# A forward part added first, a backward part scaled sooner, two buffers for B and C, and exponentials of 512 columns whose column terms TensorE sums, in the chunks of a bidirectional state-space mixer

## The chip, the cores and the metric

The program runs on 1 core of one Trainium2 chip. The metric is the device time of one execution in microseconds (us). A core has a matrix engine (TensorE, PE in the rows; PEld is its weight load), a vector engine (VectorE, DVE), an activation engine (ScalarE, ACT), a general engine (GpSimd, POOL) and a queue engine that starts most transfers (SyncE, SP). Each runs its own instructions in the order in which they are written, and they wait for one another by semaphores. Data lie in SBUF (128 partitions); TensorE writes to the eight banks of PSUM, each of 512 float32 columns.

## The reference, cut to what matters

The model has two layers over a sequence of 1024 tokens of width 1024. In each layer a state-space mixer, a gated mixer and an attention mixer read one normalised input; their outputs are joined, projected and added, and a convolutional feed-forward part follows. The change touches the state-space mixer. It works in chunks of 128 tokens, once forward and once backward, for 8 heads in 2 groups:

```python
def ssd_chunked(x, dt, a_neg, bm, cm):
    ...
    acs = jnp.cumsum((dt * a_neg).reshape(b, nc, q, g, hg), axis=2)
    seg = acs[:, :, :, None] - acs[:, :, None, :]
    decay_in = jnp.exp(jnp.where(tri[:, :, None, None], seg, NEG_INF))
    cb = jnp.einsum('bctgn,bcsgn->bctsg', cc, bc)
    y_diag = jnp.einsum('bctsg,bctsgh,bcsghp->bctghp', cb, decay_in, xdt)
    ...
    y_off = jnp.einsum('bctgn,bcghpn,bctgh->bctghp', cc, prev, jnp.exp(acs))
    return (y_diag + y_off).reshape(b, s, g, hg, p)

def ssd_mixer(xbc, z, dt_raw, conv_w, conv_b, dt_bias, a_log, d_skip, out_gain):
    ...
    y_fwd = ssd_chunked(xs, dt[:, :, 0], a_neg[0], bm, cm)
    y_bwd = flip(ssd_chunked(flip(xs), flip(dt[:, :, 1]), a_neg[1], flip(bm), flip(cm)))
    y = y_fwd + y_bwd + d_skip.astype(jnp.float32).reshape(SSD_GROUPS, hg)[..., None] * xs
    y = y.reshape(b, s, SSD_INNER) * jax.nn.silu(z.astype(jnp.float32))
    ...
```

For a chunk and a head, the exponent is a table of 128 x 128: a term of the row, a term of the column, and minus infinity where the one token may not see the other. Four such tables (the heads of a group in one direction) fill one bank of PSUM.

## The kernel before, in words

The stage that the change touches comes after attention in each layer (about 384 to 475 us in the first layer, 1611 to 1702 us in the second). First the seven backward links are computed (ra_turn, ra_state on TensorE, state_in and the loop after it on VectorE), which leaves the backward states of all chunks in BW. In the same stretch tables for the exponents are made: rows_twice writes log terms to PSUM, ScalarE copies them to MHL, and far on VectorE writes FAR (the masks) and the low halves of MHL. Then the eight chunks run in order, one after the other, each with work on four engines:

- TensorE, function chunk: the products with the carried states CURF (forward) and BW (backward), L1081, into banks 5 and 6; the exponents of group 1, which are sums(n, 2) and sums(n, 3) (each is one matrix product with FAR, L1059, and one with MHL, L1064, both over 512 columns); the gated mixer's products, L1089 and L1092; the transposes and B-C products of the next chunk, L1048 and L1051; the state of this chunk, L1104; the exponents of group 0 of the next chunk, sums(n+1, 0) and sums(n+1, 1); and last the product of the weighted table SEG with XS, L1116, one half for each group.
- ScalarE: it copies XS (L1601) and BC (L1605) out of PSUM, takes the exponentials into SEG (L1613, one instruction for each head, direction and group, as the bias differs: 16 in a chunk, of 128 columns), scales a part of the gated mixer (L1591), scales the backward product to Y2 (L1623, 8 instructions), and takes sums of squares of the chunk before (L1583).
- VectorE: it scales the forward product to Y1 (L2149) and the carried state (L2151), multiplies the gated part (L2157), then for each group adds both directions of SEG (L2143) and multiplies by the B-C table (L2144), adds the new state (L2164), and closes the chunk with L2173 and L2175.
- GpSimd, function scan: it weights XS to XW (L655), which the state product L1104 reads, makes Y3 from XS (L657), adds Y2 (L660) and then Y1 (L665); L2173 waits for the sum.

Nothing but this written order and the semaphores decides when an instruction runs; there is no planner. Chunks are called 0 to 7 here, and chunk n has n = 0 to 7. Of buffers, SEG and XS are there twice, BC, XW, Y1, Y2 and Y3 once. The second half of L1116 waits for the second L2144 (semaphore w_masked), and the next chunk's L1081 stands behind it on TensorE.

Of the kernel before, what the change touches and what calls it, by code (L numbers as in the profile page):

```python
# [19 lines left out]
F32 = mybir.dt.float32  # L20
# [5 lines left out]
P = 128  # L26
# [131 lines left out]
def trunk(nc, xT, xtok, wst, params, consts, onehot, lnrow, table, outT):  # L158
# [12 lines left out]
    with ExitStack() as ctx:  # L171
# [96 lines left out]
        ZG = place("ZG", [P, 2, 3, UC], u_at + 8192)  # L268
        JUNK = place("JUNK", [P, GROUPS, 256], u_at + 16384)
# [25 lines left out]
        BC = work("BC", [P, 2, GROUPS, P])  # L295
# [294 lines left out]
        def _(pool):  # L590
# [56 lines left out]
            def scan(l):  # L647

                for c in range(NT):
                    n, xs = l * NT + c, by_head(XS[:, c % 2])  # L650
                    pool.wait_ge(xs_ready, n + 1)
                    if c < LINKS:
                        if c:
                            pool.wait_ge(sf_full, l * LINKS + c)
                        nc.gpsimd.tensor_tensor(by_head(XW[:]), xs, per_head(WST[:, c, 0:8]), ALU.mult).then_inc(xw_ready, 1)  # L655
                    pool.wait_ge(chunk_done, 1 + n)
                    step.then(nc.gpsimd.tensor_tensor(by_head(Y3[:]), xs, per_head(par_("d_skip")), ALU.mult))  # L657
                    if c < LINKS:
                        pool.wait_ge(y2_ready, l * LINKS + c + 1)
                        ins = nc.gpsimd.tensor_tensor(Y3[:], Y3[:], Y2[:], ALU.add)  # L660
                        if c:
                            step.then(ins)
                    if c:
                        pool.wait_ge(y12_done, 1 + l * LINKS + c)
                        ins = nc.gpsimd.tensor_tensor(Y3[:], Y3[:], Y1[:], ALU.add)  # L665
                    ins.then_inc(y3_ready, 1)
# [19 lines left out]
        def _(pe):  # L686
# [167 lines left out]
            for l in range(DEPTH):  # L854
# [165 lines left out]

                def tile_in(i):
                    pe.wait_ge(xbs_full[i % 4], 16 * (l * (6, 6, 2, 1)[i % 4] + i // 4 + 1))
# [16 lines left out]
                for i in range(2, LINKS):  # L1039
                    tile_in(i)  # L1040
                    ra_turn(i)
                    pe.wait_ge(ra_t_full, l * LINKS + i + 1)
                    pe.sem_inc(xbs_used, 1)
                    ra_state(i - 1)

# [21 lines left out]

                def chunk(i2, par, end):
# [27 lines left out]
                    if not end:  # L1096
# [6 lines left out]
                        for g in range(GROUPS):  # L1103
                            last = nc.tensor.matmul(PS[:, 7, g * 256:(g + 1) * 256], BC[:, 0, g, :],  # L1104
                                                    XW[:, g * 256:(g + 1) * 256], start=True, stop=True)
# [169 lines left out]
        def _(act):  # L1275
# [121 lines left out]
            for l in range(DEPTH):  # L1397
# [154 lines left out]
                for i in range(LINKS):  # L1552
# [5 lines left out]
                    if i == 2:  # L1558
# [3 lines left out]
                        act.wait_ge(rows_full, l + 1)  # L1562
# [7 lines left out]
                        last.then_inc(far_step, 1)  # L1570
                    if 1 <= i <= 4:
# [25 lines left out]
                for c in range(NT):  # L1597
# [4 lines left out]
                    act.wait_ge(w_masked, 2 + n * 2)  # L1602
                    if c:
                        act.wait_ge(sf_full, l * LINKS + c)
                    A(BC[:].rearrange("p a g n -> p (a g n)"), bank(1), ACT.Copy).then_inc(bst_ready, 1)  # L1605
                    for j in range(4):
                        g, d = divmod(j, 2)
# [10 lines left out]
                    if c < LINKS:  # L1618
                        act.wait_ge(yo_full, n + 1)
                        act.wait_ge(chunk_done, 1 + n)  # L1620
                        for h in range(HEADS):
                            cols = slice(h * HD, (h + 1) * HD)
                            last = A(Y2[:, cols], PS[:, 6, cols], ACT.Copy, scale=EACS[:, c, 8 + h:9 + h])  # L1623
                        last.then_inc(y2_ready, 1)
# [115 lines left out]
        def _(dve):  # L1740
# [149 lines left out]
            for l in range(DEPTH):  # L1890
# [234 lines left out]
                for i2 in range(NT // 2):  # L2125
                    for par in range(2):
# [11 lines left out]
                        def masked():  # L2138

                            dve.wait_ge(bst_ready, n + 1)  # L2140
                            for g in range(GROUPS):
                                dve.wait_ge(exp_ready, 2 + n * 4 + 2 * g + 2)
                                step.then(TT(SEG[par][:, 2 * g], SEG[par][:, 2 * g], SEG[par][:, 2 * g + 1], ALU.add))  # L2143
                                TT(SEG[par][:, 2 * g], SEG[par][:, 2 * g], BC[:, 1, g, :].unsqueeze(1).to_broadcast((P, 4, P)),  # L2144
# [244 lines left out]
```

## Time and profile before

| What | us |
|---|---|
| median of 3 runs | 2486.51 (2482.69 to 2488.45) |
| time of the profiled execution | 2485.22 |
| its span | 2483.4 |
| TensorE busy | 2426.9 (98%) |
| VectorE, ScalarE, GpSimd busy | 1375.8, 998.4, 1263.1 |

The span is what the hardware profiler saw between the first and the last instruction; the execution's own time is 1.8 us longer. Busy time is the time in which an engine has an instruction running. The matmuls of TensorE overlap, each of them starting before the one ahead is through, so that a sum of their durations is more than the time that they take; the chain of waits, which gives each piece only the time that it adds, is the better ruler for them. The trace names a tile without its number, so Y is Y1, Y2 or Y3 by its line.

### The profile page before, as it was taken

The numbers are of one execution on the slowest core, as the hardware profiler recorded it, in microseconds if no ns is written. First come the engines' busy times: TensorE is split into PE (matmuls) and PEld (weight loads), VectorE is DVE, ScalarE is ACT, GpSimd is POOL, SyncE is SP. The second block draws the span as 40 slices with busy tenths as digits, with TensorE's granted clock in tenths as the row PEclk, the third lists the DMA queues.
The fourth block names the chain that finished last, engine by engine and source line by source line (L and its number), as shares of the span: only waits on it lengthen the run. The fifth ranks groups of instructions, "written<-read, shape, count | busy, mean of one in ns | idle before, by whom it ended". The sixth has DMA issues, their size and how long they took to land.

```text
span 2483.4 us, 33046 instructions
## 1 busy us (share of the span) xinstructions
PE 2426.9 (98%) x12882; PEld 2072.2 (83%) x12882; DVE 1375.8 (55%) x1561; ACT 998.4 (40%) x1737; POOL 1263.1 (51%) x814
## 2 busy tenths in 40 slices
PE   7999999999999999999999999998999999999999
PEld 6989997887888888887898899977878888888887
DVE  4476557738655546428345765586385555544332
ACT  4345567613444344212024465585144344431110
POOL 3242113323977877666633311142349877866664
PEclk9999999999999999999999999999999999999999
DMA  4434444231222212654333334442212222226544
GB/s 160 136 114 125 134 139 149 81 119 68 85 79 91 85 68 85 217 178 132 130 121 94 110 128 151 134 136 90 89 64 102 85 70 100 83 90 201 174 141 142
DMA packets 102964, 290.68 MB, mean 117 GB/s; under 512 B 7800, under 2 KB 30328, under 8 KB 101112
## 3 DMA queue, kind: packets, MB, share of 16 engines
q1 hardware_dynamic: 80360, 255.73, 30.4%
q10 hardware_dynamic: 22456, 32.90, 4.1%
q8 instruction: 103, 1.69, 0.3%
q14 instruction: 45, 0.37, 0.0%
HBM read 229.84 MB, written 58.75 MB: 116 GB/s over the span
## 4 chain that ended last, share of the span: by engine, by line
PE 81%; DVE 9%; ACT 4%; POOL 3%; issue 2%; DMA 1%; SPq 0%; ACTq 0%; DVEq 0%; POOLq 0%
PE PS L690 20%; PE PS L694 20%; PE PS L693 20%; PE PS L775 3%; PE PS L779 3%; PE PS L778 3%; PE PS L945 2%; PE PS L934 2%; POOL WL L629 2%; DVE HL L1780 1%; PE PS L1116 1%; PE PS L1081 1%; PE PS L924 1%; PE PS L923 1%; ACT LG L1501 1%
## 5 line engine op out<-in xcount | busy, mean ns | idle before, releaser
L605 POOL CAST WH<-RAW 128x1024 fp32r<-128x1024 f32 x156 | 184.5, 1182 | 905.5 <-PE PS L690 327.1
L690 PE MATMUL PS<-HH,WH 128*128 128x512 f32 x1264 | 496.4, 393 | 3.6 <-ACT QS L1668 2.6
L694 PE MATMUL PS<-HH,WL 128*128 128x512 f32 x1264 | 493.3, 390 | 0.0
L693 PE MATMUL PS<-HL,WH 128*128 128x512 f32 x1104 | 430.5, 390 | 0.0
L607 POOL TENSOR_TENSOR WL<-RAW,WH 128x1024 fp32r<-128x1024 f32 x156 | 396.8, 2543 | 12.5
L690 PEld LDWEIGHTS PS<-HH,WH 128*128 128x128 f32 x1264 | 237.4, 188 | 56.5 <-DVE HL L1780 3.5
L694 PEld LDWEIGHTS PS<-HH,WL 128*128 128x128 f32 x1264 | 237.3, 188 | 51.9
L690 PE MATMUL PS<-AR,WH 128*128 128x512 f32 x704 | 276.0, 392 | 2.3 <-DVE X L2208 1.8
L694 PE MATMUL PS<-AR,WL 128*128 128x512 f32 x704 | 275.9, 392 | 0.0
L693 PE MATMUL PS<-AR,WH 128*128 128x512 f32 x704 | 275.2, 391 | 0.0
L775 PE MATMUL PS<-WH,HH 128*128 128x256 f32 (+1 forms) x896 | 261.0, 291 | 1.7 <-ACT KN L1307 1.3
L2244 DVE TENSOR_TENSOR AR<-ARL,AR 128x512 fp32r<-128x512 f32 x88 | 136.9, 1599 | 219.3 <-ACT AR L1686 219.3
L778 PE MATMUL PS<-WL,HH 128*128 128x256 f32 (+1 forms) x896 | 254.2, 284 | 0.0
L779 PE MATMUL PS<-WH,HL 128*128 128x256 f32 (+1 forms) x896 | 254.1, 284 | 0.0
L693 PE MATMUL PS<-XL,WH 128*128 128x512 f32 x640 | 249.0, 389 | 0.0
L693 PEld LDWEIGHTS PS<-HL,WH 128*128 128x128 f32 x1104 | 207.5, 188 | 43.4
L629 POOL TENSOR_TENSOR WL<-TMP,WH 128x512 fp32r<-128x512 f32 x160 | 239.5, 1508 | 0.0
L1686 ACT ACTIVATE AR<-ARL 128x512 fp32r<-128x512 f32 x88 | 50.6, 624 | 314.5 <-DMA ARL<-act_d 314.4
L775 PEld LDWEIGHTS PS<-WH,HH 128*128 128x128 f32 x896 | 171.1, 191 | 3.0 <-issue 2.3
L778 PEld LDWEIGHTS PS<-WL,HH 128*128 128x128 f32 x896 | 171.1, 191 | 0.1
L779 PEld LDWEIGHTS PS<-WH,HL 128*128 128x128 f32 x896 | 171.0, 191 | 0.0
L1661 ACT ACTIVATE WH<-TMP 128x512 fp32r<-128x512 f32 x160 | 96.3, 628 | 166.5 <-PE PS L694 120.7
(274 smaller groups left out, 4677.3 us busy)
## 6 DMA issues: line engine op xcount, KB each, us to landing
RAW<-wst SPq DMA_DIRECT2D x156, 512.0 KB, 3.5
TOE<-toe_d SPq DMA_DIRECT2D x64, 512.0 KB, 3.7
act_d<-CVV SPq DMA_DIRECT2D x22, 1024.0 KB, 4.0
ARL<-act_d SPq DMA_DIRECT2D x88, 256.0 KB, 3.3
RAW<-wst SPq DMA_DIRECT2D x20, 1024.0 KB, 4.9
RAWB<-wst SPq DMA_DIRECT2D x20, 1024.0 KB, 4.9
XBS<-xbc_d SPq DMA_DIRECT2D x24, 512.0 KB, 4.2
xbc_d<-CV ACTq DMA_DIRECT2D x16, 512.0 KB, 3.6
```

Source lines behind the costliest of these rows:

```text
L605: nc.gpsimd.tensor_copy(hi, raw).then_inc(hi_done, 1)
L607: nc.gpsimd.tensor_tensor(lo, raw, hi.bitcast(F32), ALU.subtract).then_inc(w_ready, 1)
L629: return TT(ring(WL, s * PR + i), t, ring(WH, s * PR + i).bitcast(F32), ALU.subtract).then_inc(sw_ready, 1)
L690: ins = nc.tensor.matmul(out, wh, xh, start=first, stop=False, skip_group_check=onto)
L693: nc.tensor.matmul(out, wh, xl, start=False, stop=False, skip_group_check=onto)
L694: return nc.tensor.matmul(out, wl, xh, start=False, stop=last, skip_group_check=onto)
L775: ins = nc.tensor.matmul(o, xh, wh, start=(k == 0), stop=False)
L778: nc.tensor.matmul(o, xh, wl, start=False, stop=False)
L779: return nc.tensor.matmul(o, xl, wh, start=False, stop=(k == KT - 1))
L1661: A(ring(WH, j), (a11, s2, s1, s3, a12, s1, a22)[i], ACT.Copy).then_inc(sh_done, 1)
L1686: A(AR[:, RING[i % 8], 0], ARL[:, RING[i % 8]], ACT.Copy).then_inc(f_hi, 1)
L2244: TT(AR[:, RING[i % 8], 1], ARL[:, RING[i % 8]], AR[:, RING[i % 8], 0].bitcast(F32), ALU.subtract).then_inc(act_ready, 1)
```

## The change

Four edits, in each chunk:

1. GpSimd adds Y1 to Y3 first and Y2 second; before it was the other way round.
2. ScalarE scales the backward product to Y2 after the exponentials of group 0 and not after those of group 1.
3. BC has two buffers, one for even and one for odd chunks. The copy to BC of chunk n then waits for the chunk two back to be done with it.
4. The term that differed by head and was given as a bias of the exponential is now summed in PSUM too. NRM holds the terms (high and low parts in the upper and lower partitions), SID holds a doubled identity; one more matrix product of 512 columns in each of the four sums adds it. An exponential then takes all four heads at once, 512 columns, without a bias.

For edit 4 each layer also gets bias_rows (four matrix products in the links, after the third), one copy to NRM on ScalarE, and two instructions in far.

```diff
-        BC = work("BC", [P, 2, GROUPS, P])
+        BC = place("BC", [P, 2, 2, GROUPS, P], u_at + 25856)
...
                     step.then(nc.gpsimd.tensor_tensor(by_head(Y3[:]), xs, per_head(par_("d_skip")), ALU.mult))
+                    if c:
+                        pool.wait_ge(y12_done, 1 + l * LINKS + c)
+                        ins = nc.gpsimd.tensor_tensor(Y3[:], Y3[:], Y1[:], ALU.add)
+                        if c < LINKS:
+                            step.then(ins)
                     if c < LINKS:
                         pool.wait_ge(y2_ready, l * LINKS + c + 1)
                         ins = nc.gpsimd.tensor_tensor(Y3[:], Y3[:], Y2[:], ALU.add)
-                        if c:
-                            step.then(ins)
-                    if c:
-                        pool.wait_ge(y12_done, 1 + l * LINKS + c)
-                        ins = nc.gpsimd.tensor_tensor(Y3[:], Y3[:], Y1[:], ALU.add)
...
+                def bias_rows():
+
+                    pe.wait_ge(att_done, (l + 1) * NT)
+                    for part in range(2):
+                        for low in range(2):
+                            last = nc.tensor.matmul(PS[low * 64:low * 64 + 64, 7, (2 + part) * P:(3 + part) * P],
+                                                    NACS[:].rearrange("p c e -> p (c e)")[:, part * 64:part * 64 + 64],
+                                                    ident, start=True, stop=True, skip_group_check=True)
                     last.then_inc(rows_full, 1)
...
                         nc.tensor.matmul(bank(2 + j % 2), SEL[:, rows:rows + 1].to_broadcast((P, P)),
-                                         MHL[:, part].rearrange("p h n -> p (h n)"), start=False, stop=True,
-                                         skip_group_check=True).then_inc(ab_full, 1)
+                                         MHL[:, part].rearrange("p h n -> p (h n)"), start=False, stop=False,
+                                         skip_group_check=True)
+                        nc.tensor.matmul(bank(2 + j % 2), NRM[:, part],
+                                         SID[:, 4 * rows:4 * rows + 4].unsqueeze(2).to_broadcast((P, 4, P)),
+                                         start=False, stop=True, skip_group_check=True).then_inc(ab_full, 1)
...
-                    act.wait_ge(w_masked, 2 + n * 2)
-                    if c:
-                        act.wait_ge(sf_full, l * LINKS + c)
-                    A(BC[:].rearrange("p a g n -> p (a g n)"), bank(1), ACT.Copy).then_inc(bst_ready, 1)
+                    if n:
+                        act.wait_ge(w_masked, n * 2)
+                    if c >= 2:
+                        act.wait_ge(sf_full, l * LINKS + c - 1)
+                    A(BC[:, par].rearrange("p a g n -> p (a g n)"), bank(1), ACT.Copy).then_inc(bst_ready, 1)
...
-                        for h in range(4):
-                            e = d * 8 + g * 4 + h
-                            last = A(SEG[par][:, j, h, :], PS[:, 2 + j % 2, h * P:(h + 1) * P], ACT.Exp,
-                                     bias=NACS[:, c, e:e + 1])
-                        last.then_inc(exp_ready, 1)
+                        A(SEG[par][:, j].rearrange("p h n -> p (h n)"), bank(2 + j % 2), ACT.Exp).then_inc(exp_ready, 1)
                         if j == 1:
                             v_scaled(c)
...
+                        if j == 1 and c < LINKS:
+                                act.wait_ge(yo_full, n + 1)
+                                act.wait_ge(chunk_done, 1 + n)
...
-                    dve.wait_ge(far_step, l + 1)
+                    dve.wait_ge(far_step, 2 * l + 2)
+                    TT(SID[:], ident[:, 0:64], ident[:, 64:P], ALU.add)
+                    TT(NRM[64:P].rearrange("p a n -> p (a n)"), PS[64:P, 7, 2 * P:4 * P],
+                       NRM[64:P].rearrange("p a n -> p (a n)").bitcast(F32), ALU.subtract)
```

The order of GpSimd's instructions in chunk 1 and the start of chunk 2, before (Y_137 is Y3, Y_136 is Y2, Y_135 is Y1):

```order
L655 TENSOR_TENSOR XW<-XS,WST 128x512 [waits sf_full,xs_ready]
L657 TENSOR_TENSOR Y_137<-XS,PARM 128x512 [waits chunk_done]
L660 TENSOR_TENSOR Y_137<-Y_137,Y_136 128x512 [waits y2_ready,p_step]
L665 TENSOR_TENSOR Y_137<-Y_137,Y_135 128x512 [waits y12_done,p_step]
L655 TENSOR_TENSOR XW<-XS,WST 128x512 [waits sf_full,xs_ready]
```

and now (Y_139 is Y3, Y_138 is Y2, Y_137 is Y1):

```order
L657 TENSOR_TENSOR XW<-XS,WST 128x512 [waits sf_full,xs_ready]
L659 TENSOR_TENSOR Y_139<-XS,PARM 128x512 [waits chunk_done]
L662 TENSOR_TENSOR Y_139<-Y_139,Y_137 128x512 [waits y12_done,p_step]
L667 TENSOR_TENSOR Y_139<-Y_139,Y_138 128x512 [waits y2_ready,p_step]
L657 TENSOR_TENSOR XW<-XS,WST 128x512 [waits sf_full,xs_ready]
```

The two adds have changed places, and each keeps its own semaphore. ScalarE's instructions from the copy to BC to the squares, before (SEG_132 is the SEG of an even chunk; what follows these rows is the scaling to Y2):

```order
L1605 ACTIVATE BC<-PS 128x512 [waits sf_full,w_masked]
L1613 ACTIVATE SEG_132<-PS,NACS 128x128 [waits yd_full,ab_full]
L1613 ACTIVATE SEG_132<-PS,NACS 128x128 x3
L1613 ACTIVATE SEG_132<-PS,NACS 128x128 [waits ab_full]
L1613 ACTIVATE SEG_132<-PS,NACS 128x128 x3
L1591 ACTIVATE ST<-ST,VR 128x256
L1613 ACTIVATE SEG_132<-PS,NACS 128x128 [waits ab_full]
L1613 ACTIVATE SEG_132<-PS,NACS 128x128 x3
L1613 ACTIVATE SEG_132<-PS,NACS 128x128 [waits ab_full]
L1613 ACTIVATE SEG_132<-PS,NACS 128x128 x3
```

and now:

```order
L1626 ACTIVATE BC<-PS 128x512 [waits sf_full,w_masked]
L1631 ACTIVATE SEG_134<-PS 128x512 [waits yd_full,ab_full]
L1631 ACTIVATE SEG_134<-PS 128x512 [waits ab_full]
L1611 ACTIVATE ST<-ST,VR 128x256
L1639 ACTIVATE Y_138<-PS,EACS 128x64 [waits chunk_done,yo_full]
L1639 ACTIVATE Y_138<-PS,EACS 128x64 x7
L1631 ACTIVATE SEG_134<-PS 128x512 [waits ab_full] x2
L1603 ACTIVATE JUNK,YSS<-YT 128x256 [waits yss_ready,yz_ready]
```

Sixteen exponentials have become four, and the eight scalings to Y2 stand between the second and the third. TensorE's instructions of a chunk from the state product to the weighted product, before:

```order
L1104 MATMUL PS<-XW,BC 128x256 [waits gt_done,xw_ready,bst_ready]
L1104 MATMUL PS<-XW,BC 128x256
L1059 MATMUL PS<-FAR,IDR 128x512 [waits exp_ready]
L1064 MATMUL PS<-MHL,SEL 128x512
L1059 MATMUL PS<-FAR,IDR 128x512 [waits exp_ready]
L1064 MATMUL PS<-MHL,SEL 128x512
L1116 MATMUL PS<-XS,SEG_111 128x64 [waits w_masked,chunk_done,xs_ready]
L1116 MATMUL PS<-XS,SEG_111 128x64 x3
```

and now:

```order
L1121 MATMUL PS<-XW,BC 128x256 [waits gt_done,xw_ready,bst_ready]
L1121 MATMUL PS<-XW,BC 128x256
L1073 MATMUL PS<-FAR,IDR 128x512 [waits exp_ready]
L1078 MATMUL PS<-MHL,SEL 128x512
L1081 MATMUL PS<-SID,NRM 128x512
L1073 MATMUL PS<-FAR,IDR 128x512 [waits exp_ready]
L1078 MATMUL PS<-MHL,SEL 128x512
L1081 MATMUL PS<-SID,NRM 128x512
L1133 MATMUL PS<-XS,SEG_111 128x64 [waits w_masked,chunk_done,xs_ready]
L1133 MATMUL PS<-XS,SEG_111 128x64 x3
```

A third product stands in each of the sums; the rest is where it was.

## Rows read from the trace of the kernel before

**Rows 1.** The page, part 1: each engine's busy us and share

```profile
PE 2426.9 (98%) x12882; PEld 2072.2 (83%) x12882; DVE 1375.8 (55%) x1561; ACT 998.4 (40%) x1737; POOL 1263.1 (51%) x814
```

**Rows 2.** Busy us by window, granted clock (PEclk): a pair of chunks, two ends

```profile
415.17:432.74 17.57, 16.91 (x111) 15.46 (x111) 13.58 (x20) 16.20 (x63) 10.75 (x9) 1.00 0.30 104
...
474.00:478.00 4.00, 3.66 (x18) 3.26 (x17) 3.47 (x7) 1.33 (x2) 0.00 (x0) 0.50 0.02 6
...
1698.00:1702.00 4.00, 4.00 (x20) 4.00 (x21) 3.74 (x10) 0.21 (x1) 0.00 (x0) 0.50 0.00 0
```

**Rows 3.** Chain of waits (start us, us it adds, what) over two chunks

```profile
428.15 1.66 DVE SEG L2144
...
429.85 1.10 PE PS L1116 x8
430.96 1.78 PE PS L1081 x8
432.74 0.23 PE PS L1059
432.98 0.24 PE PS L1064
...
433.69 0.84 PE PS L1089 x8
434.52 0.17 PE PS L1092
434.69 0.66 PE PS L1048 x6
435.35 0.45 PE PS L1051 x4
435.79 0.87 PE PS L1104 x4
...
437.59 1.73 PE PS L1116 x16
```

**Rows 4.** Timeline of ScalarE, an odd chunk (start us, us, idle before)

```profile
438.12 0.72 ACT L1605 ACTIVATE BC<-PS 128x512 f32<-128x512 f32 x1
438.60 2.31 ACT L1613 ACTIVATE SEG<-PS,NACS 128x128 f32<-128x128 f32 x8
440.60 0.70 ACT L1591 ACTIVATE ST<-ST,VR 128x256 f32<-128x256 f32 x1
441.61 2.18 ACT L1613 ACTIVATE SEG<-PS,NACS 128x128 f32<-128x128 f32 x8 [0.30 <-PE PS L1064]
443.62 1.80 ACT L1623 ACTIVATE Y<-PS,EACS 128x64 f32<-128x64 f32 x8
```

**Rows 5.** Timeline of GpSimd, an even and an odd chunk

```profile
427.96 1.28 POOL L660 TENSOR_TENSOR Y<-Y,Y 128x512 f32<-128x512 f32 x1 [2.78 <-ACT Y L1623]
...
430.89 1.04 POOL L655 TENSOR_TENSOR XW<-XS,WST 128x512 f32<-128x512 f32 x1
...
437.21 1.77 POOL L660 TENSOR_TENSOR Y<-Y,Y 128x512 f32<-128x512 f32 x1 [3.83 <-ACT Y L1623]
```

**Rows 6.** Timeline of VectorE, an even chunk

```profile
428.15 1.65 DVE L2144 TENSOR_TENSOR SEG<-SEG,BC 128x512 f32<-128x512 f32 x1
...
431.03 0.69 DVE L2173 TENSOR_TENSOR Y<-Y,PS 128x512 f32<-128x512 f32 x1 [0.64 <-PE PS L1116]
```

**Rows 7.** One line's instructions, ns min/median/max: L1092, L2083

```profile
L1092 PE MATMUL PS<-GRP,BST x16: 356/356/356, 407.5 to 1694.9; 68*128 68x256 f32 x16
...
L2083 DVE SCALAR_TENSOR_TENSOR MHL<-PS,CST,MHL x8: 472/472/473, 399.4 to 1627.2; 64x256 fp32r<-64x256 f32 x8
```

**Rows 8.** Timeline: in the links, and at the last chunk

```profile
387.05 0.44 PE L1014 MATMUL PS<-PARM,CST 128*64 128x128 f32 x4
...
468.39 0.70 DVE L2143 TENSOR_TENSOR SEG<-SEG 128x512 f32<-128x512 f32 x1
...
470.91 3.33 PE L1116 MATMUL PS<-XS,SEG 128*128 128x64 f32 x16 [1.43 <-DVE SEG L2144]
```

More of the change, by code:

```diff
@@ L268, in trunk @@
         ZG = place("ZG", [P, 2, 3, UC], u_at + 8192)
+        NRM = place("NRM", [P, 2, P], u_at + 24576, F32R)
+        SID = place("SID", [P, 64], u_at + 25600, F32R)
         JUNK = place("JUNK", [P, GROUPS, 256], u_at + 16384)
@@ L1019, in rows_twice @@
                     last.then_inc(rows_full, 1)
+                def bias_rows():
[5 more added lines that the diff above has]
+                                                    ident, start=True, stop=True, skip_group_check=True)
+                    last.then_inc(rows_full, 1)
                 def tile_in(i):
@@ L1044, in _ @@
                     ra_state(i - 1)
+                    if i == 2:
+                        bias_rows()
                 def chunk_turn(i2, par):
@@ L1103, in chunk @@
                         for g in range(GROUPS):
-                            last = nc.tensor.matmul(PS[:, 7, g * 256:(g + 1) * 256], BC[:, 0, g, :],
+                            last = nc.tensor.matmul(PS[:, 7, g * 256:(g + 1) * 256], BC[:, par, 0, g, :],
                                                     XW[:, g * 256:(g + 1) * 256], start=True, stop=True)
@@ L1561, in _ @@
                         A(GRP[:], fourth, ACT.Copy)
-                        act.wait_ge(rows_full, l + 1)
+                        act.wait_ge(rows_full, 2 * l + 1)
                         for h in range(4):
@@ L1570, in _ @@
                         last.then_inc(far_step, 1)
+                    if i == 3:
+                        act.wait_ge(rows_full, 2 * l + 2)
+                        A(NRM[:].rearrange("p a n -> p (a n)"), PS[:, 7, 2 * P:4 * P], ACT.Copy).then_inc(far_step, 1)
                     if 1 <= i <= 4:
@@ L1601, in _ @@
                     A(XS[:, par], bank(0), ACT.Copy).then_inc(xs_ready, 1)
-                    act.wait_ge(w_masked, 2 + n * 2)
-                    if c:
-                        act.wait_ge(sf_full, l * LINKS + c)
-                    A(BC[:].rearrange("p a g n -> p (a g n)"), bank(1), ACT.Copy).then_inc(bst_ready, 1)
+                    if n:
[3 more added lines that the diff above has]
+                    A(BC[:, par].rearrange("p a g n -> p (a g n)"), bank(1), ACT.Copy).then_inc(bst_ready, 1)
                     for j in range(4):
-                        g, d = divmod(j, 2)
                         act.wait_ge(ab_full, 1 + n * 4 + j + 1)
@@ L1610, in _ @@
                             act.wait_ge(yd_full, n + 1)
-                        for h in range(4):
-                            e = d * 8 + g * 4 + h
-                            last = A(SEG[par][:, j, h, :], PS[:, 2 + j % 2, h * P:(h + 1) * P], ACT.Exp,
-                                     bias=NACS[:, c, e:e + 1])
-                        last.then_inc(exp_ready, 1)
+                        A(SEG[par][:, j].rearrange("p h n -> p (h n)"), bank(2 + j % 2), ACT.Exp).then_inc(exp_ready, 1)
                         if j == 1:
                             v_scaled(c)
[L1618 to L1624, printed above, removed]
+                        if j == 1 and c < LINKS:
+                                act.wait_ge(yo_full, n + 1)
+                                act.wait_ge(chunk_done, 1 + n)
+                                for h in range(HEADS):
+                                    cols = slice(h * HD, (h + 1) * HD)
+                                    last = A(Y2[:, cols], PS[:, 6, cols], ACT.Copy, scale=EACS[:, c, 8 + h:9 + h])
+                                last.then_inc(y2_ready, 1)
                     if c:
@@ L2143, in masked @@
                                 step.then(TT(SEG[par][:, 2 * g], SEG[par][:, 2 * g], SEG[par][:, 2 * g + 1], ALU.add))
-                                TT(SEG[par][:, 2 * g], SEG[par][:, 2 * g], BC[:, 1, g, :].unsqueeze(1).to_broadcast((P, 4, P)),
+                                TT(SEG[par][:, 2 * g], SEG[par][:, 2 * g], BC[:, par, 1, g, :].unsqueeze(1).to_broadcast((P, 4, P)),
                                    ALU.mult).then_inc(w_masked, 1)
```

## The prediction, made before the changed kernel ran

> **What bounds the kernel now.** I read the page first. TensorE is busy for 98% of the span, the three others for 40 to 55% [rows 1]. But that is a mean; the change lies in two stretches of some 70 us, so those count. The windows come next: a pair of chunks takes 17.57 us, and in it TensorE is busy for 16.91 and ScalarE for 16.20 [rows 2]. ScalarE looks nearly as full as TensorE, so which of them waits last has to come from the chain of waits [rows 3]. In an odd chunk the chain never leaves TensorE. Its pieces add up to 1.78 (L1081) + 0.93 (four products of two sums, 0.233 each) + 0.84 (L1089) + 0.17 (L1092) + 0.66 and 0.45 (the turn) + 0.87 (L1104) + 0.93 (the other two sums) + 1.73 (L1116) = 8.36 us. The even chunk takes the rest, 17.57 - 8.36 = 9.21. There the chain leaves TensorE once, for VectorE: the second L2144 takes 1.66, and the second half of L1116 comes late.
>
> Why 1.66, where the same instruction takes 0.69 elsewhere? The timelines put VectorE's L2144 at 428.15, just behind the start of GpSimd's L660 at 427.96, and the latter ends at 429.24; VectorE is through 0.56 later [rows 5, 6]. In the odd chunk GpSimd comes second, and its L660 takes 1.77 in place of 1.28 [rows 5]. So an add of GpSimd and an instruction of VectorE with both inputs in SBUF do not run together: whichever is second waits for the whole of the first. L2173, with one input in PSUM, takes 0.69 beside GpSimd's L655 [rows 5, 6]. The Trainium skill says the same (SBUF — State Buffer, Who interferes with whom): with two SBUF inputs VectorE contends with GpSimd, and the second blocks fully.
>
> ScalarE's row shows that it is ready just in time: in the odd chunk it waits 0.30 for TensorE [rows 4]. It doesn't set the pace.
>
> **The change part by part.** Durations are from the profiled execution, 2485.22 us, which is 1.3 under the median; differences are added to the median.
>
> *One more product in each sum.* A product of 512 columns adds 0.233 to the chain [rows 3], so four add 0.93 a chunk. TensorE's own work goes from 8.36 to 9.29. Its moving operand repeats one element 128 times, and no 512-column row does that. The nearest is L1092, whose operand repeats too: 256 columns add 0.17 [rows 3, 7], which for 512 is 0.35. Below, I know of no reason for less than 0.233, since the columns stream as in L1059. I take 0.233 and keep 0.35. The skill's figure (TensorE: Matmul & The Clock Gate, Wait — 56ns, not 53.3ns?) is 215.7 ns start to start; by it four would be an estimated 0.86, where this trace has 0.93.
>
> *Four exponentials for sixteen.* Eight of 128 columns take 2.00 from start to start of what follows (438.60 to 440.60), one copy of 512 takes 0.48 (438.12 to 438.60) [rows 4]. ScalarE's chunk goes from 16 x 0.25 to 4 x 0.48, 2.1 us less. It is not the bound, so this gives nothing by itself; the only wait for it on TensorE's way that the chain of the first layer shows before the last chunk is in chunk 0, some 0.4 us.
>
> *Two buffers for BC.* The copy no longer waits for L2144. In even chunks that wait made ScalarE late, but its exponentials were ready just before TensorE asked for them. Worth 0 on the path.
>
> *Y2 sooner, Y1 first.* Y2's eight scalings wait for L1081 and follow it at once. Counting from the end of L1081 (time 0), they end near 1.8. VectorE makes Y1 by 0.7 and scales CURF by 1.35; GpSimd's add of Y1 has to let that pass and runs from 1.25 to 2.5, and the add of Y2 follows from 2.5 to 3.8 (1.26 to 1.28 each). What was done late, beside the second L2144, is now early. The 0.85 of the even chunk goes. What is late next?
>
> I lay the engines beside one another, with 0.69 for an instruction of VectorE (0.64 in a row), 1.04 for L655, and 0.29 for a restart of TensorE after a wait (0.04 of issue and 1.10 against 0.86 [rows 3]). TensorE: two sums of 0.70 to 1.40, L1089 and L1092 to 2.41, turn to 3.52, L1104 to 4.39, two sums to 5.79, the first half of L1116 to 6.65. VectorE: L2157 from 2.5 to 2.9; L2143 is ready at 2.9 but the add of Y2 runs until 3.77; L2143 and L2144 of group 0 until 5.05. At 4.4 GpSimd asks for L655 of the next chunk. Before, it stood behind two late adds and the late copy to XS; now XS is copied near 4.1, and only L1104 holds it. It runs as soon as VectorE's instruction is through and pushes the second pair back by 0.94, to 7.27. The second half of L1116 could start at 6.65; it gets its table at 7.27, and ends at 7.27 + 0.29 + 0.86 = 8.43. With L1081 the period is 10.21. One of the two holds alone would be hidden (7.27 - 0.9 lies before 6.65); both are not.
>
> The five periods between chunks 1 and 6 were three of 8.36 and two of 9.21, 43.5; they come to 51.05: +7.5 a layer. The first period, out of chunk 0, took 9.5 by the ends of L1081 in the same chain and becomes about 9.6 by the same laying out, +0.1. The step from chunk 6 to 7 has no L655 in it: TensorE's own work is 9.29 less half of L1081 (0.89), 8.40, where the chain has 8.2 now, +0.2.
>
> *Once a layer.* bias_rows has eight passes like those of L1014, four of which take 0.44 [rows 8]: 0.4 to 0.9. TensorE has about 0.3 to spare in a link, so I take +0.2. far gets two instructions ahead of L2083, which the sums wait for and which the chain runs through: one like L2083 (0.47, in a row 0.4 [rows 7]), one of 64 columns, +0.5 together. The copy to NRM (0.38) lies beside links. The 0.47 more in the first two sums lies under the last two adds to BW.
>
> Sum for a layer: 7.5 + 0.1 + 0.2 + 0.2 + 0.5 = 8.5. Two layers: +17.0. From 2486.5 this gives **2503.5 us**.
>
> **The rivals.**
>
> *B: only TensorE's own work.* Either hold is absent, for instance because L2143 can't be held; no row shows one held, though its inputs lie in SBUF. Then the second pair is ready in time and the period is 9.29. Five are 46.45, +2.9; with the other 1.0 a layer, +7.9 together: 2494.4. By the skill's rule (same section) L2143 is held like L2144.
>
> *C: a dearer product.* At 0.35 a product, TensorE's chunk is 9.76. Under forecast A two of the four products lie inside VectorE's wait and the other two barely reach the loop; the first and last periods give about +0.6 a layer, 2504.7. Under B it adds 0.47 in 14 periods, +6.6: 2501.
>
> *D: not slower.* The place is the last chunk. TensorE waits there for VectorE (1.43 idle), and behind that the granted clock is 0.50, which is 1.2 GHz, in both layers [rows 2, 8]; L1116's sixteen pieces take 3.33 in place of 1.73. If quicker exponentials let VectorE mask sooner there, the wait and the low clock go: 2 x 1.4 of waiting, 2 x 1.6 for L1116, and about as much again for the transposes behind it and the first products of the second layer, some 11 us. Against B's +7.9 this leaves 2483. It decides as soon as the wait shrinks well under 1 us. Against it: VectorE's L2143 at 468.39 followed L2149 there, and that followed L2175 of the chunk before, not the exponentials [rows 8]; this order is kept.
>
> *E: the change frees ScalarE and ScalarE was the bound.* Then the periods would shrink towards 8.4. Against it stands a chain that stays on TensorE for a whole chunk [rows 3].
>
> **How the numbers follow.** A 0.52, B 0.25 (with shades between A and B), C 0.09, D 0.07, E 0.03, and 0.04 for something slower still, such as a clock that falls in a chunk now that TensorE waits 0.9 in each. The time is A's. The range leaves out D and E and the far end: 2492 to 2509. A measurement of this kernel can tell about 0.2%, 5 us, from no change. Slower by more than that hold A, B, C and the last, less a little of B: 0.87. Within it lie half of D and the low edge of B, 0.07. Faster: 0.06.
>
> **What would show it.** In the changed profile: four products with NRM a chunk, about 0.23 each in the chain; exponentials of about 0.6 us, and ScalarE at some 6 us a chunk with its idle time before the scalings to Y2, waiting for L1081. For A: every chunk from 1 to 5 alike at about 10.2; L2143 of group 0 ending about 0.9 late, beside the second add; a second late instruction of VectorE beside L655; and the second half of L1116 waiting about 0.6 (0.9 with its restart) in each. For B: no such wait and 9.3. If a chunk takes less than 9.2, then the price of the product is wrong; if chunks are as forecast and the total isn't, then the clock behind the last chunk is the first place to look.

## The result, and the profile after

| | before | changed |
|---|---|---|
| median of 6 runs each, us | 2484.97 (2482.69 to 2488.45) | 2504.34 (2502.08 to 2504.78) |
| ratio, 95% interval | | 1.0076 (1.0063 to 1.0088) |
| span of the profiled execution, us | 2483.4 | 2503.0 |

The changed kernel is 19.4 us slower, 19.6 by the spans. Forecast were +17.0 and 2503.5. The time came nearer to its forecast (0.8) than the difference did (2.4), and that is luck: the forecast started from 2486.5, which is 1.5 above the median of the kernel before in this comparison. First the page of the changed kernel, each engine's busy time:

```profile
PE 2443.2 (98%) x12962; PEld 2086.9 (83%) x12962; DVE 1391.2 (56%) x1565; ACT 967.7 (39%) x1547; POOL 1266.1 (51%) x814
```

Against [rows 1] ScalarE lost 31 us, as the edit meant, and the kernel lost 19. Which engine was relieved says nothing here; what the chain waits for does. The chain of waits of the changed kernel over chunk 3 (start us, us it adds, what):

```profile
437.77 1.38 ACT Y L1639 x7
...
439.36 1.14 ACT SEG L1631 x2
...
440.53 1.57 DVE SEG L2162
...
442.13 0.69 DVE SEG L2163
442.82 1.46 DVE SEG L2162
...
444.30 0.70 DVE SEG L2163
...
445.05 1.10 PE PS L1133 x8
446.15 1.80 PE PS L1098 x8
```

L1098 ends at 437.75 in one chunk and at 447.95 in the next: 10.20 us, and so it goes in every chunk from 1 to 5 (417.36 to 468.34 is 50.98 for five, 43.50 before). In [rows 3] the odd chunk never left TensorE; now every chunk goes through VectorE. Two pieces take 1.57 and 1.46 where one of their kind takes 0.69. The timeline of VectorE and GpSimd in the same chunk (start us, us, and in brackets the idle time before and its releaser) shows beside what:

```profile
440.19 0.42 DVE L2176 TENSOR_TENSOR YT<-PS,ZG 128x256 f32<-128x256 f32 x1 [1.13 <-issue]
440.27 1.27 POOL L667 TENSOR_TENSOR Y<-Y,Y 128x512 f32<-128x512 f32 x1
440.53 1.56 DVE L2162 TENSOR_TENSOR SEG<-SEG 128x512 f32<-128x512 f32 x1
442.13 0.69 DVE L2163 TENSOR_TENSOR SEG<-SEG,BC 128x512 f32<-128x512 f32 x1
442.21 1.51 POOL L657 TENSOR_TENSOR XW<-XS,WST 128x512 f32<-128x512 f32 x1 [0.67 <-PE PS L1121]
442.74 1.53 DVE L2162 TENSOR_TENSOR SEG<-SEG 128x512 f32<-128x512 f32 x1
444.30 0.69 DVE L2163 TENSOR_TENSOR SEG<-SEG,BC 128x512 f32<-128x512 f32 x1
445.05 1.10 PE L1133 MATMUL PS<-XS,SEG 128*128 128x64 f32 x8 [0.79 <-DVE SEG L2163]
```

The add of Y2, L667, starts 0.26 ahead of the first L2162 and ends at 441.54; L2162 is through 0.55 later. L657 asks while L2163 runs (1.51 in place of 1.04), and the second L2162 starts behind it and ends 0.55 after it. TensorE has done its part and waits 0.79. The chain above puts the first L2162 behind "ACT SEG L1631". Those are the exponentials of group 1, through at 440.50. The first L2162 reads group 0, whose exponentials were through by 433.85 (by ScalarE's timeline they start at 432.57 and take 1.28); what it follows is L2176, written ahead of it on VectorE, and what stretches it is L667. The one line answers for the whole kernel (ns min/median/max):

```profile
L2162 DVE TENSOR_TENSOR SEG<-SEG x32: 677/1532/1574, 410.5 to 1717.2; 128x512 f32<-128x512 f32 x32
```

Its median before was 0.683, as L2143. The new product and the exponential, by their lines:

```profile
L1081 PE MATMUL PS<-SID,NRM x64: 377/378/379, 405.3 to 1714.6; 128*128 128x512 f32 x64
```

```profile
L1631 ACT ACTIVATE SEG<-PS x64: 597/600/660, 405.7 to 1715.0; 128x512 f32<-128x512 f32 x64
```

### The profile page after: what moved, and what is told of

It reads as the page before. It is cut to its first block, busy times and chain, and to the rows that moved or that the text cites. A ratio compares the mean times of both kernels' runs of the same rounds, so it can differ in the third digit from the quotient of the medians.

```text
span 2503.0 us, 33018 instructions
## 1 busy us (share of the span) xinstructions
PE 2443.2 (98%) x12962; PEld 2086.9 (83%) x12962; DVE 1391.2 (56%) x1565; ACT 967.7 (39%) x1547; POOL 1266.1 (51%) x814
## 4 chain that ended last, share of the span: by engine, by line
PE 79%; DVE 10%; ACT 5%; POOL 3%; issue 2%; DMA 1%; SPq 0%; ACTq 0%; DVEq 0%; POOLq 0%
PE PS L692 20%; PE PS L696 20%; PE PS L695 20%; PE PS L777 3%; PE PS L781 3%; PE PS L780 3%; PE PS L947 2%; PE PS L936 2%; DVE SEG L2162 2%; POOL WL L631 2%; DVE HL L1796 1%; PE PS L1098 1%; DVE SEG L2163 1%; PE PS L926 1%; ACT LG L1518 1%
```

## The experiments

All times are against the kernel before on the same chip; its medians there were 2486.31 (first four kernels), 2486.23 (next four) and 2486.40 (last four). "After" is the changed kernel, +19.4 by its own comparison. P is the forecast's account (an instruction of GpSimd and one of VectorE hold each other up), T a rival by which TensorE's longer work sets the time, and the others are named in each text. A run whose edit adds or takes away lines has its line numbers shifted by as many against the kernel it starts from, so the addition of both directions of SEG is L2143 in before, L2162 in after, L2159 in e1 and L2163 in e2, and the product with the B-C table is the next line each time.

### The product alone: e1_no_product

After, without the third product of each sum; the column term is left out.

```diff
-                                         MHL[:, part].rearrange("p h n -> p (h n)"), start=False, stop=False,
-                                         skip_group_check=True)
-                        nc.tensor.matmul(bank(2 + j % 2), NRM[:, part],
...
+                                         MHL[:, part].rearrange("p h n -> p (h n)"), start=False, stop=True,
```

> The changed kernel without the third product in the four sums; the column term is left out of the exponent, all else (the tables for it too) is kept. Theory P (ports: the loop runs through VectorE's two pairs, held by GpSimd's add of Y2 and by the next chunk's L655-like weighting): TensorE has 0.93 us less work a chunk but waits longer before the second half of its weighted product; the period stays at about 10.1 (10.2 before the edit), so 1 to 3 us less than the changed kernel, that is about +17 to +18 us against the kernel before. Theory T (TensorE's added work is what costs): 0.93 less in each of some 15 chunk periods, 14 us less, about +5 us against the kernel before.

2505.31 (2504.01 to 2506.43), ratio 1.0076 (1.0059 to 1.0092), +19.0: hardly less than with the product, and 1 above P's number. Four products fewer in each chunk, and T's time is refuted. The period fell from 10.20 to 9.85 only, as there are still two holds: in VectorE's timeline of this kernel they are 1.65, now of group 0's product with the table and not of its addition, and 1.53.

```profile
441.43 1.65 DVE L2160 TENSOR_TENSOR SEG<-SEG,BC 128x512 f32<-128x512 f32 x1
443.00 1.53 DVE L2159 TENSOR_TENSOR SEG<-SEG 128x512 f32<-128x512 f32 x1
```

Those 0.35 are 3.5 us in ten periods, and they are not in the total. One chunk of each layer took 11.5. The window of this kernel that holds it (columns as in [rows 2]; the two beside it have 1.00), and TensorE's timeline in it:

```profile
434.00:444.00 10.00, 9.96 (x54) 8.66 (x54) 6.60 (x9) 5.61 (x19) 6.23 (x4) 0.83 0.31 92
```

```profile
433.79 1.62 PE L1130 MATMUL PS<-XS,SEG 128*128 128x64 f32 x8 [1.01 <-DVE SEG L2160]
...
445.31 1.10 PE L1130 MATMUL PS<-XS,SEG 128*128 128x64 f32 x8 [1.01 <-DVE SEG L2160]
```

TensorE with less work waits longer, 1.01 in place of 0.79, and behind one such wait the mean granted clock of a window fell from 1.00 to 0.83 (it is 0.55 from 434 to 436, so most of that at 1.2 GHz), which made the eight pieces 1.62 in place of 1.10 and the chunk 1.67 longer. Twice 1.67 eats the 3.5.

### XW moved out of the way: e2_xw_late

After, and L657 waits until the second pair of VectorE is through.

```diff
+                            pool.wait_ge(w_masked, 2 + n * 2)
```

> The changed kernel, but GpSimd weights XS to XW only after VectorE is through with both pairs of the chunk before, so that it can't run beside them. P: the second hold goes (0.94), TensorE's own work decides, the period is 9.3: 5 us a layer less than the changed kernel, about +9 to +10 us against the kernel before, and no wait before the second half of the weighted product in chunks 1 to 5. T: an added wait changes nothing or costs, +19 or more.

2495.81 (2495.16 to 2498.61), ratio 1.0040 (1.0025 to 1.0054), +9.5. One more wait makes the changed kernel 9.9 us faster. The chain of this kernel, one chunk from L1099 to L1099, is TensorE alone, 9.35 us:

```profile
442.59 1.78 PE PS L1099 x8
...
450.06 1.88 PE PS L1134 x16
451.94 0.27 PE PS L1099
```

The add of Y2 still holds L2163 (1.56 at 447.17), and this is nearly hidden: L1134 takes 1.88 in place of 1.73. So this hold alone is nearly hidden, and the two together are not. The other one alone was not run.

### The adds as they were: e3_old_adds

After, without edit 1.

```diff
-                        pool.wait_ge(y12_done, 1 + l * LINKS + c)
-                        ins = nc.gpsimd.tensor_tensor(Y3[:], Y3[:], Y1[:], ALU.add)
...
                         ins = nc.gpsimd.tensor_tensor(Y3[:], Y3[:], Y2[:], ALU.add)
...
+                        pool.wait_ge(y12_done, 1 + l * LINKS + c)
+                        ins = nc.gpsimd.tensor_tensor(Y3[:], Y3[:], Y1[:], ALU.add)
```

> The changed kernel with GpSimd's adds in the old order, Y2 first and then Y1 (edit 1 undone). P: the add of Y2 has to wait for its scalings (1.8 after L1081's end), so both adds come later and hold VectorE for longer; laid out, the period is 10.76 in place of 10.21, 3.3 us a layer: about +26 us against the kernel before. T: no difference, +19.

2513.03 (2511.82 to 2514.99), ratio 1.0105 (1.0089 to 1.0122), +26.7: the period is 10.56 (12.23 and 11.74 in two chunks of the second layer, at a lower clock), with three holds in the chain of this kernel, the first of them short. P's +26 was hit in part by luck: it laid out a period of 10.76, and the two slow chunks, 2.9 us together, made up for most of the difference. Edit 1 is a gain inside the change.

```profile
442.60 0.97 DVE SEG L2162
...
443.60 1.65 DVE SEG L2163
445.25 1.46 DVE SEG L2162
```

### The first three edits: e4_edits123

Before with edits 1 to 3, exponentials and sums as before. The scalings are where the change puts them:

```diff
-                    if c < LINKS:
+                        if j == 1 and c < LINKS:
                             act.wait_ge(yo_full, n + 1)
```

> The kernel before with edits 1, 2 and 3 (Y1 added first, Y2 scaled sooner, two buffers for BC), and with the old sixteen exponentials and two products in each sum. P: GpSimd's early add and early weighting stand beside VectorE's pairs here too; laid out, the period is 10.1 and the sum about +16 to +17 us against the kernel before, with no work added on TensorE at all. T: without the third product nothing costs; the even chunk's wait may go, -5 to 0 us.

2502.68 (2500.02 to 2505.03), ratio 1.0064 (1.0047 to 1.0081), +16.4. Nearly the whole loss is there without the new product. The period is 9.75, TensorE waits 0.90 in each, and of the ten, two took 11.4 at a clock of 0.83. VectorE is held twice in a chunk here too, both times in the product with the table:

```profile
441.60 1.65 DVE L2145 TENSOR_TENSOR SEG<-SEG,BC 128x512 f32<-128x512 f32 x1
...
443.89 1.45 DVE L2145 TENSOR_TENSOR SEG<-SEG,BC 128x512 f32<-128x512 f32 x1
```

P had laid out 10.1. Its number came true because the two slow chunks (3.4 us together) made up for the shorter period (3.5 us in ten), which it had not foreseen.

### Edit 1 by itself: e5_y1_first

Before, with the two adds changed over.

```diff
+                        ins = nc.gpsimd.tensor_tensor(Y3[:], Y3[:], Y1[:], ALU.add)
...
                         ins = nc.gpsimd.tensor_tensor(Y3[:], Y3[:], Y2[:], ALU.add)
...
-                        ins = nc.gpsimd.tensor_tensor(Y3[:], Y3[:], Y1[:], ALU.add)
```

> The kernel before with edit 1 alone: GpSimd adds Y1 first, then Y2. P: the add of Y2 still comes late (its scalings stand behind all exponentials) and now always beside VectorE's second pair, since the add of Y1 is out of its way: the alternation of 8.36 and 9.21 becomes 9.2 in every chunk, 2.2 us a layer, about +4 us against the kernel before. Rival (the even chunk's wait comes from the two adds being late together, so that doing one early takes it away): the period goes to 8.36, -5 us.

2480.76 (2478.47 to 2483.05), ratio 0.9980 (0.9971 to 0.9990), -5.5: P's +4 missed, and the rival's -5 (the even chunk's wait came from the two adds being late together) was met. The odd chunk's 8.35 became the period of all. VectorE and GpSimd in this kernel:

```profile
434.74 0.69 DVE L2144 TENSOR_TENSOR SEG<-SEG,BC 128x512 f32<-128x512 f32 x1
```

```profile
434.77 1.78 POOL L665 TENSOR_TENSOR Y<-Y,Y 128x512 f32<-128x512 f32 x1 [1.98 <-ACT Y L1623]
```

The add of Y2 comes 0.03 to 0.04 us behind the start of L2144 in every chunk, so GpSimd is held (1.78) and TensorE is not. I had laid it just ahead. In the even chunks of before the add was 0.19 ahead, at 427.96 against 428.15 [rows 5, 6], and it cost 0.85. The mechanism stands, as the add held here is the second of the two, but which comes first was decided by less than my laying out can tell.

### And its order made sure: e6_y1_first_y2_masked

Edit 1, and the add of Y2 starts only when VectorE is through with both pairs (w_masked).

```diff
                         pool.wait_ge(y2_ready, l * LINKS + c + 1)
+                        pool.wait_ge(w_masked, 2 + n * 2 + 2)
                         ins = nc.gpsimd.tensor_tensor(Y3[:], Y3[:], Y2[:], ALU.add)
```

> The kernel before with edit 1 and one more wait: GpSimd adds Y2 only when VectorE is through with both pairs of the chunk. P: no instruction of GpSimd runs beside a pair any more, TensorE's own 8.36 decides every chunk, 3 us a layer less: about -6 us against the kernel before (-3 to -7). Rival: the add of Y2 becomes so late that L2173 and with it the next chunk wait for it: 0 to +5.

2479.60 (2477.56 to 2481.38), ratio 0.9975 (0.9965 to 0.9985), -6.6: the fastest version, ahead of both kernels. It is not to be told from e5, but it doesn't hang on 0.03 us. GpSimd's add takes 1.26, as it meets nobody:

```profile
446.30 1.26 POOL L666 TENSOR_TENSOR Y<-Y,Y 128x512 f32<-128x512 f32 x1 [2.81 <-DVE SEG L2145]
```

### The same wait in the changed kernel: e7_after_y2_masked

```diff
+                        pool.wait_ge(w_masked, 2 + n * 2 + 2)
```

> The changed kernel with that same wait before the add of Y2. As the next chunk's weighting stands behind this add on GpSimd, both holds go. P: TensorE's own 9.29 decides, as with the late weighting alone: about +9 to +10 us against the kernel before. T: no gain, +19.

2492.86 (2491.75 to 2494.60), ratio 1.0030 (1.0019 to 1.0041), +6.6. Both instructions of GpSimd now run outside VectorE's two pairs; the chunk takes 9.20, all on TensorE, and 12.8 of the 19.4 us are back. P had +9 to +10 by a period of 9.29; the shorter one makes 0.9 of the 3 us that it missed by, and the rest was not looked into. The third products (L1082) add 0.21 to 0.22 each in its chain:

```profile
444.12 0.23 PE PS L1079
444.35 0.22 PE PS L1082
```

### The last chunk: e8_last_chunk_too

e6, and the last chunk's add of Y1 waits for the mask as well.

```diff
+                        if c == LINKS:
+                            pool.wait_ge(w_masked, 2 + n * 2 + 2)
```

> The kernel of the run with edit 1 and the wait before the add of Y2, and in the last chunk of a layer the add of Y1 waits for VectorE's pairs as well. P: L2144 of group 0 is no longer held there, TensorE waits about 0.5 in place of 1.4 before the last weighted products. If the low clock behind it follows from that wait, the clock stays at 2.4 GHz and 2 to 5 us a layer go: -10 to -16 us against the kernel before. If it comes from something else (VectorE's normalising, the waits of the transposes), only the wait itself goes: 1 us a layer less than the other kernel, about -8.

2480.70 (2476.79 to 2483.29), ratio 0.9977 (0.9968 to 0.9986), -5.5: nothing beyond e6, where -8 or more was expected. TensorE's timeline at its end:

```profile
467.89 1.08 PE L1119 MATMUL PS<-XS,SEG 128*128 128x64 f32 x8 [0.47 <-DVE SEG L2147]
469.61 1.97 PE L1119 MATMUL PS<-XS,SEG 128*128 128x64 f32 x8 [0.64 <-DVE SEG L2147]
```

The wait went from 1.43 [rows 8] (1.40 in e6) to 0.47 and 0.64, the second behind exponentials that came late, and the clock fell all the same (0.50 from 470 to 474). So that wait alone isn't what brings the clock down there, and what does stays open. The second layer of the changed kernel, in the next section, has the opposite case, a wait of 1.44 with the full clock behind it.

### Edits 2, 3 and 4 apart

e9_y2_late: after, with edit 2 undone, the scalings behind the exponentials of group 1.

```diff
-                        if j == 1 and c < LINKS:
+                    if c < LINKS:
```

> The changed kernel with edit 2 undone: the scalings to Y2 stand behind all four exponentials again. P: the add of Y2 comes later and holds a later instruction of VectorE; laid out, the period is 10.49 in place of 10.21, 2.5 us a layer: about +24 us against the kernel before. If, as with edit 1 alone, the add and the pair miss one another by some hundredths, it could be +14 instead. T: no difference, +19.

2506.91 (2505.36 to 2507.85), ratio 1.0084 (1.0068 to 1.0099), +20.5, between P's two numbers, +24 and +14, and no farther from T's +19. So the time alone doesn't tell the two accounts apart here; the timeline does: the add of Y2 is 1.57 long, 0.27 behind L2163 of group 0, so that GpSimd is held first; but it and L657 behind it then lie in front of both instructions of group 1. Two holds again, other ones, and a period of 10.29.

```profile
443.30 0.69 DVE L2163 TENSOR_TENSOR SEG<-SEG,BC 128x512 f32<-128x512 f32 x1
443.91 1.78 DVE L2162 TENSOR_TENSOR SEG<-SEG 128x512 f32<-128x512 f32 x1
445.72 1.42 DVE L2163 TENSOR_TENSOR SEG<-SEG,BC 128x512 f32<-128x512 f32 x1
```

```profile
443.57 1.57 POOL L667 TENSOR_TENSOR Y<-Y,Y 128x512 f32<-128x512 f32 x1 [1.32 <-ACT Y L1639]
445.10 1.49 POOL L657 TENSOR_TENSOR XW<-XS,WST 128x512 f32<-128x512 f32 x1
```

e10_one_bc: after, with one BC and the waits of before.

```diff
-        BC = place("BC", [P, 2, 2, GROUPS, P], u_at + 25856)
+        BC = work("BC", [P, 2, GROUPS, P])
```

> The changed kernel with edit 3 undone: one buffer for BC, whose copy waits for the chunk before again. P: the copy is not on the way, since ScalarE has over 3 us to spare a chunk: 0 to +1 against the changed kernel, +19 to +20 against the kernel before.

2504.64 (2501.53 to 2507.77), ratio 1.0069 (1.0054 to 1.0085), +18.2; period 10.20, as in after. Edit 3 does nothing that can be measured.

e11_edits123_y2_masked: e4 with the wait of e6, that is e7 without edit 4.

```diff
+                        pool.wait_ge(w_masked, 2 + n * 2 + 2)
```

> The kernel before with edits 1, 2 and 3, and the add of Y2 only after VectorE's pairs. P: with nothing of GpSimd beside a pair the period is TensorE's own 8.36, as in the kernel with edit 1 and this wait: -5 to -8 us against the kernel before, where without the wait the same three edits cost 16. The difference to the changed kernel with this wait (+6.6) is then the price of edit 4 by itself, 12 to 14 us: 0.93 in 14 to 16 periods of a chunk less one or two for faster exponentials in the last, and 1.2 a layer for its tables. T has no forecast of its own here.

2480.63 (2479.24 to 2482.84), ratio 0.9977 (0.9968 to 0.9986), -5.8, period 8.34. Free of holds, edits 2 and 3 add nothing to edit 1, and edit 4 costs the difference to e7, 12.4 us: 8.6 of them by ten periods of 9.20 in place of 8.34. With the holds there, edit 4 costs only what lies between e4 and after, 3.0 us, since its products then fall in large part into TensorE's wait.

e12_edit4_alone: before with edit 4 alone.

```diff
+                        A(SEG[par][:, j].rearrange("p h n -> p (h n)"), bank(2 + j % 2), ACT.Exp).then_inc(exp_ready, 1)
```

> The kernel before with edit 4 alone (third product, four exponentials, the tables). P: laid out, the add of Y2 now begins beside VectorE's first pair, the add of Y1 beside the second, and the next weighting behind it; the period is 10.7, 12.6 us a layer and 1.2 for the tables: +24 to +28 us against the kernel before. T: TensorE's 0.93 a chunk less the even chunk's wait, as ScalarE is relieved: +10 to +16.

2514.28 (2512.80 to 2515.78), ratio 1.0110 (1.0095 to 1.0126), +27.9, P's number; T's +10 to +16 is refuted. The chain has both of group 1's instructions held in every chunk, and TensorE waits 1.10. Three of the five periods of a layer are 10.51, where P laid out 10.7; the first two are 11.81 and 10.88 (11.96 and 10.73 in the second layer), with a stretch at the low clock, and bring the time to the top of P's range:

```profile
444.43 1.71 DVE SEG L2161
446.16 1.65 DVE SEG L2162
```

## Why the prediction was right

Its likeliest case happened, by its mechanism, and the total is 2.4 us above the forecast's difference. The excess is not in the ten periods, which were right, but in the small terms around them. Both holds are in every chunk from 1 to 5 (the two fences of the changed kernel above), where before one hold came in every second chunk. That the time is theirs and not the product's was shown from four sides: taking one hold away (e2) gives back 9.9 of the 19.4 us, taking both (e7) 12.8, taking the product away 0.4; and the other three edits alone (e4) lose 16.4. The two causes don't add up, though. What is left in e7, +6.6, is what edit 4 costs (12.4) less what the other edits gain once nothing is held (5.8, e11).

Term by term for the first layer. These rows are windows of before and of after, from the end of the carried product of chunk 1 to that of chunk 6, and from there to the transposes of the next part:

```profile
415.17:458.67 43.50, 42.17 (x276) 38.61 (x276) 32.70 (x49) 40.40 (x156) 26.02 (x20) 1.00 0.31 107
458.67:486.32 27.65, 22.59 (x129) 19.69 (x128) 23.91 (x40) 17.85 (x55) 7.70 (x6) 0.88 0.05 15
```

```profile
417.36:468.34 50.98, 47.05 (x296) 42.55 (x296) 39.98 (x50) 30.68 (x95) 29.54 (x21) 1.00 0.26 91
468.34:496.78 28.44, 24.95 (x135) 21.85 (x135) 23.23 (x38) 14.60 (x36) 6.49 (x5) 0.82 0.05 15
```

- *Chunks 1 to 5*: +7.48, forecast +7.5. The wait of the second half was 0.79, forecast "about 0.6 (0.9 with its restart)".
- *The product*: 0.22 in the chain, forecast 0.233. That its operand repeats one element 128 times costs nothing; C's 0.35 is out.
- *Once a layer*: +1.2, forecast +0.7. This is a mis-sized term. The eight passes of bias_rows went to the path whole. The link behind them starts at 393.67, before at 392.56; the links began 0.37 later, which leaves 0.74 where 0.2 was forecast. TensorE's timeline there:

```profile
390.87 1.10 PE L1006 MATMUL PS<-XWA,BSTA 128*128 128x256 f32 x4 [0.30 <-DVE BW L2118]
391.90 0.66 PE L1028 MATMUL PS<-CST,NACS 128*64 128x128 f32 x8
392.49 0.87 PE L995 MATMUL PS<-CST,XBR 128*128 128x128 f32 x6
393.67 1.10 PE L1006 MATMUL PS<-XWA,BSTA 128*128 128x256 f32 x4 [0.31 <-PE PS L995]
```

  The time between two links was not free as I took it to be. The turn, L995, lies in it, and the link now waits for the turn instead of for VectorE. The two instructions of far took 0.22 and 0.43, and came to +0.5 as forecast.
- *Chunk 0*: +0.6, forecast +0.1, mis-sized too. L1109 comes 0.20 later than the terms above make it, as two more products stand ahead of it; L2176 starts 0.92 behind the start of L1109 where it was 0.57, for which the trace shows no reason (0.56 in the second layer, where chunk 0 was longer all the same); and VectorE's two pairs then take 0.15 more, being held twice, by the add of Y2 and by L657, where it was once. No experiment isolates this; it is read from the trace alone.

```profile
410.20 0.42 DVE L2176 TENSOR_TENSOR YT<-PS,ZG 128x256 f32<-128x256 f32 x1 [1.72 <-PE PS L1109]
410.55 0.94 DVE L2162 TENSOR_TENSOR SEG<-SEG 128x512 f32<-128x512 f32 x1
```

- *From chunk 6 on*: +0.79, forecast +0.2. The last chunk's wait and slow product are what they were (1.44 and 3.21; [rows 8] 1.43 and 3.33), so D did not happen in this layer. What is longer is the piece behind it: all sixteen of the next transposes ran at the low clock, 3.90, where before the last eight took 1.11 at the full one.

In the second layer half of D did happen. The last chunk's rows there, before and after:

```profile
1697.88 3.65 PE L1116 MATMUL PS<-XS,SEG 128*128 128x64 f32 x16 [2.67 <-DVE SEG L2144]
```

```profile
1717.42 1.08 PE L1133 MATMUL PS<-XS,SEG 128*128 128x64 f32 x8 [1.44 <-DVE SEG L2163]
1718.66 1.10 PE L1133 MATMUL PS<-XS,SEG 128*128 128x64 f32 x8 [0.16 <-DVE SEG L2163]
```

The wait shrank and the sixteen pieces ran at the full clock. But the clock fell later, over the transposes (0.50 from 1724 to 1732), and from chunk 6 to the same place as above this layer was still 0.5 longer than before. So D's place was read rightly; the low clock moved and did not go, and its 11 us did not come.

The first layer's terms add up to 1.2 + 0.6 + 7.5 + 0.8 = 10.1, and the second layer added 9.1, in part as its step from chunk 6 to 7 was slower before (8.56 in place of 8.17, from one L2149 to the next). Together with the 0.4 at the start of the links this is the 19.6 of the spans.

B fell by its premise: L2143 can be held, and as L2162 it is (1.56 and 1.53 in the changed kernel, and the same line in e1, e2 and e3). E fell with the page: ScalarE got 31 us back and waits 3.5 us a chunk for L1098. C fell with the product's 0.22. The small last case, a clock that falls inside the chunks, did not show in the changed kernel but did in e1, e3, e4 and e12. It is why e1 gained next to nothing and e4 only 3.0 us over the changed kernel, and a forecast that only adds up the waits would have missed it there.

The step that failed outright was not in the prediction but in the expectation for e5: the same laying out, carried to an order that hung on 0.03 us.

## What to carry to other kernels

Where GpSimd runs beside instructions of VectorE with both inputs in SBUF, write down for each chunk which of the two asks first, and what TensorE waits for behind it. A wait on GpSimd that lets VectorE's critical pair go first was worth 12.8 us in the changed kernel. In the kernel before it came with the adds changed over, 6.6 us together, of which the change of order alone gave 5.5; what the wait adds there is too small to measure, but the order no longer hangs on 0.03 us. In neither kernel did the wait cost anything, as GpSimd had time to spare. Relieving an engine that isn't the bound (ScalarE, 31 us less) brought nothing here, and the work that it was traded for landed on the engine that is: 12.4 us for edit 4 even where nothing was held. A hold that is nearly hidden alone (e2) can cost much together with a second one, so test them one at a time and together.

## What the runs showed of the hardware

- *A hold is to the end of the other's instruction.* In the changed kernel an instruction of VectorE with both inputs in SBUF ended 0.55 us after the instruction of GpSimd that it met (the add of Y2, then the weighting), twice in every chunk (441.54 to 442.09, 443.72 to 444.27). In return GpSimd's L657 grew from 1.04 to 1.51 behind L2163. The order was decided by 0.03 us in e5 and by 0.19 in before. These rows agree with the rule that the prediction took from the Trainium skill (SBUF — State Buffer, Who interferes with whom), now for L2143 too.
- *A clock that falls inside a loop.* In the profiled executions, kernels in which TensorE waited 0.90 (e4), 1.01 (e1, e3) or 1.10 us (e12) in each chunk had a stretch of low granted clock (0.83 in the 10 us window of e1) in two of ten chunks, which were 1.2 to 1.7 us longer than the others; those with 0.79 (after), 0.80 (e10) and 0.88 (e9) had none, in ten chunks each. That is one execution of each and no rule: the last chunk of the changed kernel's second layer waited 1.44 and ran on at the full clock, and e8's clock fell behind waits of 0.47 and 0.64.
- *A moving operand that repeats one element streamed like the others here*: 0.378 long and 0.22 from start to start for 512 columns, beside 0.23 for L1073 and L1078.
- *One exponential of 512 columns from PSUM takes 0.60*, and two in a row 1.13; the same columns in eight instructions with a bias took 2.31 [rows 4].
